# Two mixers' attention normalized on GpSimd before the transposes, values as stationary rows, and the order of work in the first and later mixers changed

## The chip, the cores and the metric

One core of one Trainium2 chip. The metric is device time in microseconds (us) of one launch; its median over several runs is what is compared. A "turn" below is a transpose on TensorE (a matmul against the identity); PSUM banks are written as numbers 0 to 7.

## What is computed

Four layers on 256 rows of width 1,024, in float32. The kernel runs them in one launch:

```python
for layer in range(2):                       # first block
    hn  = rms_norm(x, norm_mix_pre[layer])
    mix = even_mixer(...) if layer == 0 else odd_mixer(...)   # attention + state space; gated recurrence
    x   = x + rms_norm(mix, norm_mix_post[layer])
    x   = x + rms_norm(swiglu(rms_norm(x, ...)), ...)
for i in range(2):                           # second block
    h = _rmsnorm(x, norm_mix[i])
    # i == 0: 8 heads, scores from two parts (128 + 64 wide); i == 1: 8 heads that share 2 key/value heads
    # both: 4 more heads against a memory of 256 rows
    s = q @ k.T ; p = softmax(s * scale) ; out = p @ v
    x = x + concat(mix, mem_out) @ w_out[i]
    x = x + swiglu(_rmsnorm(x, norm_ffn[i]))
```

The change is in the first mixer (its first projection and its state space), in small orders of the second and third, and above all in the attention of the third and fourth mixers: 12 heads each, 256 queries by 256 keys, values 128 wide.

## The kernel before

**Precision and weights.** Every projection is done as three matmuls on rounded parts (`mm3`, L458 to L461): high by high, high input by the weight's rest, and the input's rest by the high weight. Weights come in chunks of 128 x 2,048 (1 MB each) through three buffers RAW (SyncE's queue, `weights`), are rounded by ScalarE into WH (`split_hi`, L1098) and their rest is taken by VectorE into WL (`split_lo`, L1715). `feed(c)` on ScalarE and on VectorE does this for the chunks up to c + 3; where it stands in each engine's program is written by hand. One such feed occupies VectorE for over 2 us.

**Order.** Each engine runs one in-order program (`pe`, `act`, `dve`, `pool`, `sync`), all cross-engine order is by semaphores that the programs wait on. An instruction that waits holds everything behind it on its engine.

**Attention of the third and fourth mixers** (`attention_ahead`, one function in each of `pe`, `act`, `dve`). For each head h:

- TensorE `products(h)` (L759): scores of 256 x 256 into bank h % 2; the third mixer's own heads take two parts, so twice the matmuls.
- VectorE `top(h)` (L2273): the row maxima, negated.
- ScalarE (L1583): the exponentials into P (two buffers), with their row sums into `den`.
- TensorE `turn_p(h)` (L465): P is turned into bank 2 + h % 2.
- VectorE (L2295): the copy of that bank into PT.
- TensorE `pv(h)` (L783): PT by the values; queries are output rows. Four matmuls with 128 columns.
- After each four heads: VectorE `group_divide` (`divide`, L2028 and L2034) divides by the sums into Y, TensorE `finish` turns Y (8 turns for each group), ScalarE copies it rounded (`attn_group`, L1115), VectorE takes the rest (`group_lo`, L1731), and these are the inputs of the output projection `wide_mm`.

TensorE's program for one step of `attend` is `products(h + 2)`, `turn_p(h)`, fill, `pv(h - 1)`. VectorE's is `top(h + 2)`, copy of h, `fill(h)`, and divide or lo where due. The fills are what the rest of the mixer still owes: turns of further queries and keys on TensorE; on VectorE scaled evacuations and feeds (`fill2`: h = 0, 1, 3, 7; `fill3`: h = 0, 1, 3, 7). GpSimd does only the small inverse roots of the norms (`rsqrt`, L2405 and L2407) in this stage.

**First mixer.** `first_edge` does the first projection, beginning when row 0's turned and rounded inputs and the chunk's first quarter are split in both parts. The state space goes in four quarters q: TensorE `b_u(q)`, VectorE `rotate(q)` and `scan(q)` (L1975 to L1997), which ends with two products W, then TensorE `c_h(q)` (L670 to L675) into bank 7, then VectorE `skip(q)` (L1962), which reads bank 7. GpSimd computes CFe from CFo (L2463 to L2470).

Of the kernel before, what the change touches and what calls it, by code (L numbers as in the profile page):

```python
# [212 lines left out]
class Tally:  # L213
# [5 lines left out]
    def up(self):  # L219
# [9 lines left out]
    qk mx ex tp pta ptd pv yt ytp oh ol glua glud  # L229
# [8 lines left out]
              ("n1", 1), ("nk1", 1), ("g0", 8), ("g2", 4), ("g1", 8), ("g3", 8))  # L238
# [4 lines left out]
HSUM = numbered("memk0 n0 nk0 zm qp memk1 n1 nk1")  # L243
# [3 lines left out]
def program(nc, A, PLAN, NCH):  # L247
# [10 lines left out]
    with top:  # L258
# [146 lines left out]
        PD = numbered("R TH a1 a2 a3 a4 a5 THE PH AA AB DEN REC R2 SN CS h1 h2 h3 AB_ CSm p q s FR r u v FI f1 f2 f3 CF")  # L405
# [11 lines left out]
        FFNS = ("ffn0", "ffn1", "ffn2", "ffn3")  # L417
        WHEN = (3, 5, 5, 5, 5, 3, 3, 3)
# [12 lines left out]
        def htlo_n(ed, t, k):  # L431
            return 16 * ed + 8 * t + k + 1
# [24 lines left out]
        def pe(e):  # L457
# [40 lines left out]
            def first_edge():  # L498

                for c in range(2):  # L500
                    for t in range(2):
                        for i in range(4):
                            k = 4 * c + i
                            if t == 0 and c == 0:
                                e.wait_ge(S.lo, i + 1)
                            elif t == 0 and i == 0:
                                e.wait_ge(S.lo1, 1)
                            elif t == 0 and i == 2:
                                e.wait_ge(S.lo, 5)
                            tk = edge_product(0, c, PS[:, t, :], t, k, slice(512 * i, 512 * i + 512))  # L510
                            if c == 0 and t == 0 and i == 0:
                                e.wait_ge(S.c_x1, 16)
                                turn(0, 1, (0,))
                            elif c == 0 and t == 1 and i == 0:
                                turn(0, 1, (1,))
                    tk.then_inc(S.used, 1)
# [144 lines left out]
            def c_h(q):  # L661
                if q == 0:
                    e.wait_ge(S.k0, 1)
                    e.wait_ge(S.pp, PP["CF"])
                else:
                    e.wait_ge(S.ssm, q)
                e.wait_ge(S.w, 2 * q + 2)
                for j in range(4):
                    rows = slice(32 * j, 32 * j + 32)
                    e.matmul(PS[rows, 7, 0:128], K0[rows, q, :], uT[rows, q, 0:256:2], start=True, stop=False)  # L670
                for i in range(4):
                    for j in range(4):
                        e.matmul(PS[32 * j:32 * j + 32, 7, 128:256], CFo[:, i // 2, 4 * q + j, :], W[:, WAT[i], JJ[j], :], start=False, stop=False)
                    for j in range(4):
                        tk = e.matmul(PS[32 * j:32 * j + 32, 7, 1:128], CFe[:, i // 2, 4 * q + j, :], W[:, WAT[i], JJ[j], 0:127], start=False, stop=i == 3)  # L675
                tk.then_inc(S.ch, 1)
# [17 lines left out]
            def attention0():  # L694
# [23 lines left out]
                def pv(h):  # L718
                    e.wait_ge(S.pta, h + 1)
                    if h == 4:  # L720
                        e.wait_ge(S.yt, 2)
# [28 lines left out]
            def attention_ahead(base, heads, P, PT, Y, ready, fill, pvfree, tfree=None):  # L750
# [24 lines left out]
                def pv(h):  # L775
# [4 lines left out]
                    for t in range(2):  # L780
                        b, o = heads[h]["banks"][t], heads[h]["at"]
                        for kt in range(2):
                            tk = e.matmul(PS[:, b, o:o + 128], PT[:, h % 2, kt, 128 * t:128 * t + 128], heads[h]["v"][kt],  # L783
                                          start=kt == 0, stop=kt == 1)
                    tk.then_inc(S.pv, 1)

                def finish(h0):
                    G = (base + h0) // 4
                    for jp in range(2):
                        four(heads[h0]["banks"][jp], Y, jp,  # L790
                             lambda j, t: e.wait_ge(S.yt, 2 * G + t + 1) if j == 0 and jp == 0 else None).then_inc(S.ytp, 1)

                def attend():
                    for h in range(13):
# [7 lines left out]
                        if h in (5, 9):  # L802
                            finish(h - 5)

                return products, attend, finish
# [222 lines left out]
            def tfree2():  # L1028
# [3 lines left out]
            products2, attend2, finish2 = attention_ahead(8, HEADS2, P2, PT2, Y2, ready2, fill2, pvfree2, tfree2)  # L1032
# [5 lines left out]
                    at={0: [lambda: mem_rows(1, mem_free, (0, 1))], 1: [lambda: mem_rows(1, mem_free, (2, 3))]})  # L1038
# [13 lines left out]
            wide_mm(PLAN["out0"], 5, lambda k: (YAh, YAl, OUT0[k // 2] + k % 2), lambda ci: e.wait_ge(S.ol, 3 + ci), lambda: finish2(8))  # L1052
# [30 lines left out]
            products3, attend3, finish3 = attention_ahead(20, HEADS3, P3, PT3, Y3, ready3, fill3, pvfree3)  # L1083
# [6 lines left out]
            wide_mm(PLAN["out1"], 7, lambda k: (YAh, YAl, k), lambda ci: e.wait_ge(S.ol, 9 + ci), lambda: finish3(8))  # L1090
# [3 lines left out]
        def act(e):  # L1094
# [25 lines left out]
            def turn(ed, t, then=None):  # L1120
                name, gi = GAINS[ed]
                ts = slice(128 * t, 128 * t + 128)
                for j in range(2):
                    e.wait_ge(S.turn, turn_n(ed, t, j))
                    for i in range(4):
                        k = 4 * j + i
                        copy(HTh[:, k, ts], PS[:, 4 + 2 * t + j, 128 * i:128 * i + 128], col(name, gi + k)).then_inc(S.hthi, 1)
# [142 lines left out]
            turn(0, 0, lambda j: first_split(j))  # L1270
            first_split(2)
            first_split(3)

            def second_split(j):
                if j == 0:
                    e.wait_ge(S.w1, 16)
                    e.activation(WH[:, 1, 0:1024], RAW[:, 1, 0:1024], ACT.Copy).then_inc(S.hi1, 1)
                    split_hi(1, slice(1024, CH))
                    n_split[0] = 2

            turn(0, 1, second_split)
# [41 lines left out]
            def decay_sines():  # L1323
                e.wait_ge(S.pd, PD["DEN"])
                e.wait_ge(S.fills, 2)
                e.activation(N1, THE, ACT.Abs).then_inc(S.pa, 1)
                e.activation(SN, THE, ACT.Sin).then_inc(S.pa, 1)
                e.wait_ge(S.pa, PA["N1"])
                e.activation(CS, N1, ACT.Sin, bias=hp[:, 0:1], scale=-1.0).then_inc(S.pa, 1)

# [16 lines left out]
            decay_sines()  # L1347
# [362 lines left out]
        def dve(e):  # L1710
# [26 lines left out]
            def turn(ed, t, then=None):  # L1737
                name, gi = GAINS[ed]
                ts = slice(128 * t, 128 * t + 128)
                for j in range(2):  # L1740
                    e.wait_ge(S.hthi, htlo_n(ed, t, 4 * j + 3))
                    for i in range(4):
                        k = 4 * j + i
                        rest(HTl[:, k, ts], PS[:, 4 + 2 * t + j, 128 * i:128 * i + 128], HTh[:, k, ts], col(name, gi + k)).then_inc(S.htlo, 1)
# [136 lines left out]
            turn(0, 0, first_split)  # L1881
            first_split(2)
            first_split(3)

            def second_split(j):
                if j == 0:
                    e.wait_ge(S.hi1, 1)
                    e.tensor_tensor(WL[:, 1, 0:1024], RAW[:, 1, 0:1024], WH[:, 1, 0:1024].bitcast(f32), SUB).then_inc(S.lo1, 1)
                    e.wait_ge(S.hi, 5)
                    split_lo(1, slice(1024, CH))  # L1890
                    n_split[0] = 2

            turn(0, 1, second_split)
# [6 lines left out]
            feed(PLAN["ev_u"][0] - 1)  # L1900
            e.wait_ge(S.pa, PA["SN"])
            e.tensor_tensor(SN, SN, R, MUL).then_inc(S.pd, pd.up())
            e.wait_ge(S.pa, PA["CS"])
# [715 lines left out]
```

## Time and profile before

| | |
|---|---|
| median of 3 runs | 1256.16 us (1255.80 to 1256.63) |
| profiled execution | 1257.03 us, of which the span is 1255.2 us |
| TensorE busy | 1237.0 us, 6,366 matmuls |
| VectorE busy | 810.8 us |
| ScalarE busy | 670.5 us |
| GpSimd busy | 91.0 us |
| granted TensorE clock, mean | 1.000 |

How to read it: busy time is the union of the intervals in which an engine has an instruction in flight, and matmuls overlap, so a matmul's duration is longer than the time it holds TensorE. Between two matmuls of one kind, the distance from start to start is what each costs. A float32 matmul (not rounded) shows as two instructions in the trace, a turn as one. A row of the time line gives start, duration, engine, line, operation, output and inputs, shape, how many like instructions were merged, and in brackets the idle time before it with what ended it.

### The profile page before, as it was taken

How to read it: one execution, taken by the hardware profiler on the slowest of the kernel's cores; microseconds unless marked ns; L12 is line 12 of the kernel's file. 1: busy time of each engine (PE TensorE's matmuls, PEld its weight loads, DVE VectorE, ACT ScalarE, POOL GpSimd, SP SyncE). 2: the span in 40 equal slices, each digit the busy share in tenths (PEclk: the TensorE clock that was granted, in tenths of full speed). 3: DMA queues.
4: the chain of work that ended last, by engine and by line, in shares of the span. 5: the costliest groups of instructions: out<-in, count | busy, mean ns of one | idle time of the engine just before them, and what ended most of it. 6: DMA issues, size and time to landing. Idle time of an engine off the chain costs nothing.

```text
span 1255.2 us, 15794 instructions
## 1 busy us (share of the span) xinstructions
PE 1237.0 (99%) x6366; PEld 1030.9 (82%) x6366; DVE 810.8 (65%) x1034; ACT 670.5 (53%) x981; POOL 91.0 (7%) x121
## 2 busy tenths in 40 slices
PE   7999999999999999999999999999999999999998
PEld 6778888888888888888888888888888888888887
DVE  7995766654787766654687756656547774655553
ACT  7765644433898644443687635444436654544431
POOL 2410100000110100000133100000001200000000
PEclk9999999999999999999999999999999999999999
DMA  7334555555554565555554124555555334555551
GB/s 302 102 116 145 194 188 197 179 191 200 186 200 145 193 219 198 175 194 188 187 201 169 67 102 167 201 186 183 182 192 183 126 102 137 199 182 187 187 183 67
DMA packets 32392, 216.60 MB, mean 173 GB/s; under 512 B 3888, under 2 KB 4272, under 8 KB 7232
## 3 DMA queue, kind: packets, MB, share of 16 engines
q1 hardware_dynamic: 30240, 210.19, 48.5%
q0 software_dynamic: 1360, 4.78, 1.2%
q8 instruction: 50, 0.82, 0.3%
q10 hardware_dynamic: 720, 0.63, 0.2%
q14 instruction: 22, 0.18, 0.0%
HBM read 214.54 MB, written 1.05 MB: 172 GB/s over the span
## 4 chain that ended last, share of the span: by engine, by line
PE 89%; DVE 7%; issue 1%; ACT 1%; POOL 1%; DMA 0%; DVEq 0%; SPq 0%; ACTq 0%
PE PS L459 25%; PE PS L461 25%; PE PS L460 25%; PE PS L465 5%; PE PS L759 2%; DVE WL L1715 1%; PE PS L493 1%; PE PS L496 1%; PE PS L494 1%; PE PS L783 1%; PE PS L533 1%; PE PS L527 1%; PE PS L528 1%; DVE YG L1992 1%; DVE YG L1982 0%
## 5 line engine op out<-in xcount | busy, mean ns | idle before, releaser
L1715 DVE TENSOR_TENSOR WL<-RAW,WH 128x2048 fp32r<-128x2048 f32 (+2 forms) x200 | 443.1, 2218 | 310.9 <-ACT WH L1098 310.9
L1098 ACT ACTIVATE WH<-RAW 128x2048 fp32r<-128x2048 f32 (+2 forms) x200 | 370.7, 1857 | 367.2 <-PE PS L461 367.2
L459 PE MATMUL PS<-WH,HTh 128*128 128x512 f32 (+1 forms) x848 | 334.7, 395 | 0.1
L461 PE MATMUL PS<-WH,HTl 128*128 128x512 f32 (+1 forms) x848 | 329.0, 388 | 0.0
L460 PE MATMUL PS<-WL,HTh 128*128 128x512 f32 (+1 forms) x848 | 328.3, 387 | 0.0
L461 PEld LDWEIGHTS PS<-WH,HTl 128*128 128x128 f32 x848 | 159.2, 188 | 33.2
L459 PEld LDWEIGHTS PS<-WH,HTh 128*128 128x128 f32 x848 | 159.4, 188 | 32.1 <-DVE WL L1715 1.1
L460 PEld LDWEIGHTS PS<-WL,HTh 128*128 128x128 f32 x848 | 159.5, 188 | 30.6
L459 PE MATMUL PS<-WH,YAh 128*128 128x512 f32 x402 | 158.8, 395 | 0.4 <-DVE HTl L1732 0.3
L461 PE MATMUL PS<-WH,YAl 128*128 128x512 f32 x402 | 156.7, 390 | 0.0
L460 PE MATMUL PS<-WL,YAh 128*128 128x512 f32 x402 | 156.5, 389 | 0.0
L459 PEld LDWEIGHTS PS<-WH,YAh 128*128 128x128 f32 x402 | 75.5, 188 | 16.2 <-issue 1.5
L461 PEld LDWEIGHTS PS<-WH,YAl 128*128 128x128 f32 x402 | 75.5, 188 | 15.9
L460 PEld LDWEIGHTS PS<-WL,YAh 128*128 128x128 f32 x402 | 75.6, 188 | 14.9
L2405 POOL TENSOR_SCALAR st<-st 128x2 f32<-128x2 f32 (+4 forms) x33 | 20.2, 611 | 761.4 <-ACT JK L1133 699.3
L459 PE MATMUL PS<-WH,YBh 128*128 128x512 f32 x160 | 62.5, 391 | 0.0
L461 PE MATMUL PS<-WH,YBl 128*128 128x512 f32 x160 | 62.3, 389 | 0.0
L460 PE MATMUL PS<-WL,YBh 128*128 128x512 f32 x160 | 62.3, 389 | 0.0
L1115 ACT ACTIVATE HTh<-PS,cst 128x128 fp32r<-128x128 f32 (+1 forms) x136 | 39.0, 377 | 25.5 <-PE PS L465 25.5
L1732 DVE SCALAR_TENSOR_TENSOR HTl<-PS,cst,HTh 128x128 fp32r<-128x128 f32 (+1 forms) x136 | 38.9, 351 | 14.0 <-ACT HTh L1115 13.9
L2407 POOL TENSOR_TENSOR st<-st,mh 128x2 f32<-128x2 f32 (+4 forms) x33 | 39.6, 1201 | 2.7
L1115 ACT ACTIVATE YAh<-PS 128x512 fp32r<-128x512 f32 x38 | 21.6, 584 | 29.1 <-PE PS L465 29.1
(344 smaller groups left out, 1445.2 us busy)
## 6 DMA issues: line engine op xcount, KB each, us to landing
RAW<-in_w SPq DMA_DIRECT2D x196, 1024.0 KB, 4.9
BC<-in_rows POOLq DMA_DIRECT2D x4, 512.0 KB, 4.0
YG<-in_mem POOLq DMA_DIRECT2D x4, 512.0 KB, 4.9
X<-in_x SPq DMA_DIRECT2D x2, 512.0 KB, 5.6
RAW<-in_w SPq DMA_DIRECT2D x4, 256.0 KB, 5.8
BC<-in_s SPq DMA_DIRECT2D x1, 512.0 KB, 11.8
YG<-in_s SPq DMA_DIRECT2D x1, 512.0 KB, 12.0
BB<-in_s SPq DMA_DIRECT2D x1, 512.0 KB, 12.7
```

Of the source, the lines that this page charges most:

```text
L459: e.matmul(out, ah, bh, start=start, stop=False)
L460: e.matmul(out, ah, bl, start=False, stop=False)
L461: return e.matmul(out, al, bh, start=False, stop=stop)
L465: return e.transpose(out, src, ident[0:p, 0:p])
L493: e.matmul(out, HTh[:, k, ts], WH[:, c % NW, w], start=k == 0, stop=False)
L759: tk = e.matmul(PS[:, h % 2, 256 * t:256 * t + 256], q[:, 128 * t:128 * t + 128], k[:, 0:256], start=i == 0, stop=i == len(parts) - 1)
L1098: e.activation(WH[:, c % NW, w], RAW[:, c % NR, w], ACT.Copy).then_inc(S.hi, 1)
L1115: return e.activation(out, src, ACT.Copy, scale=scale)
L1715: e.tensor_tensor(WL[:, c % NW, w], RAW[:, c % NR, w], WH[:, c % NW, w].bitcast(f32), SUB).then_inc(S.lo, 1)
L1732: return e.scalar_tensor_tensor(out, src, gain, hi.bitcast(f32), MUL, SUB)
L2405: e.tensor_scalar(st[:, at:at + n], st[:, at:at + n], 1e-6, None, ADD).then_inc(S.var, 1)
L2407: e.tensor_tensor(st[:, at:at + n], st[:, at:at + n], mh[:, 0:n], ALU.pow).then_inc(S.rs, 1)
```

## The change

In the attention of the third and fourth mixers:

- VectorE takes the reciprocal of a head's sums at once (12 small ones instead of 3 of four heads each), in its program ahead of `top(h + 2)` and so behind `fill(h - 1)`.
- GpSimd multiplies P of that head (128 x 512) in place by it (`norm`). TensorE's `turn_p(h)` waits for this (`S.pn`) instead of for the exponentials.
- `pv` has the values as the stationary operand and PT as the moving one: two matmuls with 256 columns for four with 128; the output is already turned. `group_divide`, Y and `finish` are gone.
- In the fourth mixer the squares of one group of queries go from ScalarE to VectorE (`memory_squares`), VectorE's feeds there from h = 0, 1, 7 to h = 7 and later.

In the first mixer: the first projection begins with the products that need only the high part, other turns are interleaved, `decay_sines` and `factor` come earlier, `c_h` waits for W half by half and q = 2 uses bank 6, so `skip(2)` moves into the attention. In the second mixer `conv(3)` and `conv_parts(1)` go ahead of a feed and a squares operation; in the third the second half of `mem_rows` goes one step ahead.

```diff
@@ pe
             def first_edge():
-                for c in range(2):
-                    for t in range(2):
-                        for i in range(4):
...
+                for i in range(4):
+                    w = slice(512 * i, 512 * i + 512)
+                    e.wait_ge(S.hthi, htlo_n(0, 0, i))
+                    e.wait_ge(S.hi, i + 1)
+                    e.matmul(PS[:, 0, :], HTh[:, i, 0:128], WH[:, 0, w], start=i == 0, stop=False)
+                    e.wait_ge(S.htlo, htlo_n(0, 0, i))
+                    e.matmul(PS[:, 0, :], HTl[:, i, 0:128], WH[:, 0, w], start=False, stop=False)
...
+                for i in range(4):
+                    e.wait_ge(S.lo, i + 1)
+                    e.matmul(PS[:, 0, :], HTh[:, i, 0:128], WL[:, 0, 512 * i:512 * i + 512], start=False, stop=False)
...
             def c_h(q):
+                b = CH_BANK[q]
                 if q == 0:
                     e.wait_ge(S.k0, 1)
-                    e.wait_ge(S.pp, PP["CF"])
-                else:
-                    e.wait_ge(S.ssm, q)
-                e.wait_ge(S.w, 2 * q + 2)
+                elif q != 2:
+                    e.wait_ge(S.ssm, q - q // 3)
...
+                for n, i in enumerate((0, 3, 1, 2)):
+                    if n % 2 == 0:
+                        e.wait_ge(S.w, 2 * q + 1 + n // 2)
...
                 def turn_p(h):
...
+                    e.wait_ge(S.pn, base - 8 + h + 1)
                     for t in range(2):
-                        e.wait_ge(S.ex, 2 * (base + h) + t + 1)
...
                 def pv(h):
...
-                    for t in range(2):
-                        b, o = heads[h]["banks"][t], heads[h]["at"]
-                        for kt in range(2):
-                            tk = e.matmul(PS[:, b, o:o + 128], PT[:, h % 2, kt, 128 * t:128 * t + 128], heads[h]["v"][kt],
-                                          start=kt == 0, stop=kt == 1)
+                    b, o = heads[h]["banks"][h % 4 // 2], 256 * (h % 2)
+                    for kt in range(2):
+                        tk = e.matmul(PS[:, b, o:o + 256], heads[h]["v"][kt], PT[:, h % 2, kt, :], start=kt == 0, stop=kt == 1)
                     tk.then_inc(S.pv, 1)
-                def finish(h0):
...
-                        if h in (5, 9):
-                            finish(h - 5)
...
             rows_mm(PLAN["qb0"], 3, 3, 512, CQ, (2, 3), qb0_ready,
-                    at={0: [lambda: mem_rows(1, mem_free, (0, 1))], 1: [lambda: mem_rows(1, mem_free, (2, 3))]})
+                    at={0: [lambda: mem_rows(1, mem_free, (0, 1)), lambda: mem_rows(1, mem_free, (2, 3))]})
@@ act
             mem_k(0, (0, 1), KZ)
-            feed(PLAN["mem00"][1])
+            conv_parts(1)
...
+            feed(PLAN["mem00"][1])
             e.wait_ge(S.lamd, 1)
-            conv_parts(1)
...
             def attn_group(base, heads, g, at):
                 for jp in range(2):
-                    attn_out(2 + 2 * ((base - 8) // 4 + g) + jp + 1, heads[4 * g]["banks"][jp], at + 2 * jp)
+                    e.wait_ge(S.pv, base + 4 * g + 2 * jp + 2)
+                    copy(YAh[:, at + 2 * jp:at + 2 * jp + 2, :], pair(heads[4 * g]["banks"][jp])).then_inc(S.oh, 1)
...
-                    e.wait_ge(S.hsq, HSQ["g1"] + 8)
-                    head_norm("g3", two(Zg[3]), 4, 128, "g3")
@@ dve
-            factor()
             table(0)
...
             rotate(3)
-            skip(2)
             scan(3)
...
+            conv(3)
             feed(PLAN["mem00"][0])
-            conv(3)
...
-                for h in range(13):
+                for h in range(12):
+                    e.wait_ge(S.ex, 2 * (base + h) + 2)
+                    e.reciprocal(den[:, :, h:h + 1], den[:, :, h:h + 1]).then_inc(S.rd, 1)
                     if h + 2 < 12:
                         top(h + 2)
...
                     fill(h)
-                    if h % 4 == 0 and h:
-                        group_divide(h // 4 - 1)
-                    elif h in (6, 10):
+                    if h in (6, 10):
                         group_lo(h // 4 - 1)
...
+            def memory_squares(z):
+                sq = BC[:, :].rearrange("p (a b) -> p a b", a=2)
+                e.wait_ge(S.z, ZEV["g3"] + 2)
+                e.wait_ge(S.dv, dv.n)
+                e.scalar_tensor_tensor(sq, z, 1.0 / 128, z, MUL, MUL).then_inc(S.dv, dv.up())
+                e.wait_ge(S.dv, dv.n)
+                e.tensor_reduce(st[:, SO["g3"]:SO["g3"] + 8], sq.rearrange("p a (h d) -> p (a h) d", d=128), AX.X, ADD).then_inc(S.hsum, 1)
             def fill3(h):
-                if h == 0:
-                    feed(PLAN["gqa1"][1])
-                elif h == 1:
-                    feed(PLAN["gqa3"][0])
+                if h == 1:
+                    memory_squares(Zg[3][:, :, :])
                 elif h == 3:
                     scaled("g3", two(Zg[3]), 4, 128)
                 elif h == 7:
-                    feed(PLAN["gqa3"][1])
+                    feed(PLAN["gqa1"][1])
...
+            feed(PLAN["gqa3"][0])
@@ pool
+            def norm(base, P, den, hs):
+                for h in hs:
+                    e.wait_ge(S.rd, base - 8 + h + 1)
+                    e.tensor_tensor(P[:, h % 2, :, :], P[:, h % 2, :, :], den[:, :, h:h + 1].to_broadcast([128, 2, 256]), MUL).then_inc(S.pn, 1)
...
             head_rsqrt("nk1", 8)
+            norm(8, P2, den2, range(12))
...
             head_rsqrt("g1", 8)
+            norm(20, P3, den3, range(4))
             head_rsqrt("g3", 8)
+            norm(20, P3, den3, range(4, 12))
```

## Rows read from the trace of the kernel before

**Rows 1.** The page's first part: busy time, share and instructions of each engine.
```profile
PE 1237.0 (99%) x6366; PEld 1030.9 (82%) x6366; DVE 810.8 (65%) x1034; ACT 670.5 (53%) x981; POOL 91.0 (7%) x121
```

**Rows 2.** Busy time by stretch: span, each engine (instructions), clock, DMA share, GB/s.
```profile
690.00:731.00 41.00, 40.80 (x268) 36.59 (x267) 30.66 (x44) 22.26 (x62) 3.81 (x4) 1.00 0.22 78
1000.00:1031.00 31.00, 29.76 (x218) 26.80 (x216) 26.58 (x38) 20.11 (x70) 2.65 (x2) 1.00 0.30 102
```

**Rows 3.** Time line of TensorE in the fourth mixer's attention: start, duration, instruction.
```profile
1000.78 0.60 PE L465 MATMUL PS<-ident,A3P 128*128 128x128 f32 x4
...
1016.35 1.03 PE L759 MATMUL PS<-KM,QMg 128*128 128x256 f32 x4
1017.21 0.60 PE L465 MATMUL PS<-ident,A3P 128*128 128x128 f32 x4
1017.65 1.06 PE L783 MATMUL PS<-Zg,A3PT 128*128 128x128 f32 x8
1018.54 1.03 PE L759 MATMUL PS<-KM,QMg 128*128 128x256 f32 x4
...
1030.98 0.48 PE L459 MATMUL PS<-WH,YAh 128*128 128x512 f32 x1
```

**Rows 4.** The same of the third mixer's attention.
```profile
698.41 0.60 PE L465 MATMUL PS<-ident,Z 128*128 128x128 f32 x4
...
717.13 0.60 PE L759 MATMUL PS<-KTn,QTn 128*128 128x256 f32 x2
...
718.86 0.60 PE L465 MATMUL PS<-ident,Z 128*128 128x128 f32 x4
...
731.27 0.48 PE L459 MATMUL PS<-WH,YAh 128*128 128x512 f32 x1
```

**Rows 5.** Time line of VectorE in the fourth mixer's attention.
```profile
1012.63 0.19 DVE L2028 RECIPROCAL A3den<-A3den 128x8 f32<-128x8 f32 x1
...
1017.41 0.69 DVE L2273 TENSOR_REDUCE A3M<-PS 128x2 f32<-128x512 f32 x1 [1.46 <-PE PS L759]
1018.02 0.68 DVE L2295 COPY A3PT<-PS 128x512 f32<-128x512 f32 x1
1018.62 1.28 DVE L1731 TENSOR_TENSOR YAl<-PS,YAh 128x512 fp32r<-128x512 f32 x2
...
1021.01 2.28 DVE L1715 TENSOR_TENSOR WL<-RAW,WH 128x2048 fp32r<-128x2048 f32 x1
```

**Rows 6.** Time line of ScalarE: the first of one head's two exponentials.
```profile
1008.50 0.47 ACT L1583 ACTIVATE A3P<-PS,A3M 128x256 f32<-128x256 f32 x1 [0.70 <-DVE A3M L2273]
```

**Rows 7.** Time line of GpSimd: CFe in the first mixer, a root in the fourth.
```profile
33.79 1.05 POOL L2463 TENSOR_TENSOR CFe<-CFo,s 128x512 f32<-128x512 f32 x1 [7.75 <-DVE CFo L1946]
...
37.18 3.10 POOL L2467 TENSOR_TENSOR CFe<-CFo,s 128x512 f32<-128x512 f32 x1
...
1008.05 1.66 POOL L2407 TENSOR_TENSOR st<-st,mh 128x8 f32<-128x8 f32 x1
```

**Rows 8.** Time line of VectorE beside that, and at the end of the last quarter.
```profile
36.53 2.85 DVE L1715 TENSOR_TENSOR WL<-RAW,WH 128x2048 fp32r<-128x2048 f32 x1
...
78.77 0.47 DVE L1962 SCALAR_TENSOR_TENSOR yq<-uT,cst,PS 128x256 f32<-128x256 f32 x1
...
82.74 1.22 DVE L1997 TENSOR_TENSOR W<-YG,SX 128x1024 f32<-128x1024 f32 x1
```

**Rows 9.** Time line of TensorE in the first mixer: first product, and two `c_h`.
```profile
9.30 0.79 PE L493 MATMUL PS<-WH,HTh 128*128 128x512 f32 x1 [2.13 <-DVE WL L1715]
...
51.32 0.43 PE L670 MATMUL PS<-uT,K 32*32 32x128 f32 x8 [1.26 <-DVE W L1997]
...
84.10 0.43 PE L670 MATMUL PS<-uT,K 32*32 32x128 f32 x8 [1.22 <-DVE W L1997]
```

**Rows 10.** Time line of TensorE: one wait each in the second and third mixer.
```profile
360.89 0.36 PE L459 MATMUL PS<-YAh,WH 128*128 128x256 f32 x1 [0.61 <-issue]
...
647.35 0.47 PE L459 MATMUL PS<-WH,YAh 128*128 128x512 f32 x1 [0.33 <-DVE HTl L1732]
```

More of the change, by code:

```diff
@@ L498, in first_edge @@
             def first_edge():
[L500 to L516 removed]
+                for i in range(4):
[5 more added lines that the diff above has]
+                    e.matmul(PS[:, 0, :], HTl[:, i, 0:128], WH[:, 0, w], start=False, stop=False)
+                    if i == 1:
+                        e.wait_ge(S.c_x1, 16)
+                        turn(0, 1, (0,))
+                    elif i == 3:
+                        turn(0, 1, (1,))
@@ L748, in attention0, with attention_ahead @@
                 return finish
-            def attention_ahead(base, heads, P, PT, Y, ready, fill, pvfree, tfree=None):
+            def attention_ahead(base, heads, P, PT, ready, fill, pvfree, tfree=None):
                 def products(h):
@@ L801, in attend @@
                             pv(h - 1)
-                        if h in (5, 9):
-                            finish(h - 5)
-                return products, attend, finish
+                return products, attend
             def gain_turn(src, name, bks, free=None, tiles=4):
@@ L1118, in act, with turn_half, turn @@
                      ("norm_mix_2", 0), ("norm_ffn_2", 0), ("norm_mix_2", 8), ("norm_ffn_2", 8))
-            def turn(ed, t, then=None):
+            def turn_half(ed, t, j):
                 name, gi = GAINS[ed]
                 ts = slice(128 * t, 128 * t + 128)
+                e.wait_ge(S.turn, turn_n(ed, t, j))
+                for i in range(4):
+                    k = 4 * j + i
+                    copy(HTh[:, k, ts], PS[:, 4 + 2 * t + j, 128 * i:128 * i + 128], col(name, gi + k)).then_inc(S.hthi, 1)
+            def turn(ed, t, then=None):
                 for j in range(2):
[L1124 to L1127, printed above, removed]
+                    turn_half(ed, t, j)
                     if then:
@@ L1268, in first_split, with decay_sines @@
                 split_hi(0, slice(512 * i, 512 * i + 512))
[L1270 to L1281, printed above, removed]
+            def decay_sines():
+                e.wait_ge(S.pd, PD["DEN"])
+                e.wait_ge(S.fills, 2)
+                e.activation(N1, THE, ACT.Abs).then_inc(S.pa, 1)
+                e.activation(SN, THE, ACT.Sin).then_inc(S.pa, 1)
+                e.wait_ge(S.pa, PA["N1"])
+                e.activation(CS, N1, ACT.Sin, bias=hp[:, 0:1], scale=-1.0).then_inc(S.pa, 1)
+            turn_half(0, 0, 0)
+            for i in range(4):
+                first_split(i)
+            decay_sines()
+            turn_half(0, 1, 0)
+            turn_half(0, 0, 1)
+            e.wait_ge(S.w1, 16)
+            e.activation(WH[:, 1, 0:1024], RAW[:, 1, 0:1024], ACT.Copy).then_inc(S.hi1, 1)
+            split_hi(1, slice(1024, CH))
+            n_split[0] = 2
+            turn_half(0, 1, 1)
             def angles(q):
@@ L1735, in dve, with turn_half, turn @@
                      ("norm_mix_2", 0), ("norm_ffn_2", 0), ("norm_mix_2", 8), ("norm_ffn_2", 8))
-            def turn(ed, t, then=None):
+            def turn_half(ed, t, j):
                 name, gi = GAINS[ed]
                 ts = slice(128 * t, 128 * t + 128)
+                e.wait_ge(S.hthi, htlo_n(ed, t, 4 * j + 3))
+                for i in range(4):
+                    k = 4 * j + i
+                    rest(HTl[:, k, ts], PS[:, 4 + 2 * t + j, 128 * i:128 * i + 128], HTh[:, k, ts], col(name, gi + k)).then_inc(S.htlo, 1)
+            def turn(ed, t, then=None):
                 for j in range(2):
[L1741 to L1744, printed above, removed]
+                    turn_half(ed, t, j)
                     if then:
@@ L2040, in step @@
                     if h == 2:
+                        skip(2)
                         skip(3)
@@ L2268, in dve, with attention_ahead @@
             two = lambda Z: [Z[:, t, :] for t in range(2)]
-            def attention_ahead(base, heads, M, den, PT, Y, fill, at):
+            def attention_ahead(base, heads, M, den, PT, fill, at):
                 def top(h):
```

122 lines of the change are left out of this document (62 added, 60 removed).

## The prediction

> **What bounds the kernel now.** I read the page's first part, then busy time by stretch, then the time lines of the two attentions. TensorE is busy 1237.0 of 1255.2 us [rows 1]: elsewhere only matmuls that go away, or waits of TensorE, can shorten the kernel. In the attentions TensorE is still busy 40.8 of 41.0 us and 29.8 of 31.0 us, but VectorE has 30.7 and 26.6 us of work there [rows 2], so little need be hung between the two to make a wait. The clock is granted in full in both. The reader should see in [rows 3] how TensorE passes from one head's step to the next without a hole, though each step depends on three engines. It can, because `turn_p(h)` needs only exponentials that were done long before.
>
> **What goes from TensorE.** `finish` is 8 turns; 4 take 0.44 us (1017.21 to 1017.65) [rows 3], so 0.87; three in each mixer, so 2.6 us each, of which the last, 0.87 us, lies in the output projection. `pv` of a head takes 0.89 us (1017.65 to 1018.54) for four matmuls of 128 columns. `products` of a plain head is two matmuls of 256 columns in 0.86 us (1016.35 to 1017.21), and the new `pv` has just that shape: 0.87, a gain of 0.02, 0.5 us over 24 heads. If TensorE stayed the bound, this would be 5.7 us.
>
> **What comes in: a ring.** The reciprocal of head h + 1 stands behind VectorE's copy and fill of head h. GpSimd's multiplication waits for it, `turn_p(h + 1)` waits for that, and the copy of h + 1 waits for the turn. So from turn to turn there is now a closed loop through three engines:
>
> - turn: 0.44 us (1017.21 to 1017.65) [rows 3];
> - to VectorE: 0.20 us, as from the end of the products at 1017.21 to the maximum at 1017.41 [rows 3, 5];
> - copy: 0.60 us (1018.02 to 1018.62) [rows 5];
> - VectorE's fill of that head, D;
> - reciprocal: 0.19 us for 8 columns [rows 5], with its handover 0.25;
> - multiplication on GpSimd: 1.05 us for the same 128 x 512 with a broadcast operand [rows 7], with handover 1.15 (0.10 is my estimate, of the size of the handover to ScalarE).
>
> Sum 2.64 us + D. TensorE's own work for a head is 0.86 + 0.44 + 0.87 = 2.17 in the fourth mixer and for the third mixer's memory heads; its own heads have products of 1.73 us (717.13 to 718.86) [rows 4], so 3.04. A plain head therefore stalls 0.5 us even without a fill, the two last heads of each mixer, which have no products ahead, 1.3 us, and every fill on VectorE enters in full unless products or turns cover it. Before, the copy of h was wanted only after `products(h + 2)` and `turn_p(h + 1)`, which hid D.
>
> The fills are: a feed 2.2 us, a pair of scaled evacuations or rests 1.2 us [rows 5], two operations of `memory_squares` on 1,024 columns, half a feed each and some 0.1 over, 2.4 us.
>
> I laid out both attentions head by head in this way, each engine in its program's order, with 1.05 us for a head's exponentials, two of 0.47 and the reading of their sums [rows 6] (0.91 before ScalarE is free for its next), and an operation of VectorE with two SBUF inputs excluding one of GpSimd. The same layout of the old programs gives 731.2 and 1030.9 us for the start of the output projections; the trace has 731.27 and 1030.98 [rows 3, 4]. For the new programs the distances from turn to turn are:
>
> - Fourth mixer, from head 0: 2.8, 5.0 (squares), 2.6, 4.6 (scaling of g3, 1.2, behind GpSimd's root, which follows `norm` of head 3: 0.3 and 1.66 us [rows 7]), 3.0 and 2.8 (TensorE or ScalarE last), 3.8 (rests), 4.8 (feed), 2.6, 2.6, 3.8 (rests), and 2.2 to the projection: 40.9 us. Before: 1000.78 to 1030.98, 30.2 us. So +10.7, less the `finish` of 0.87 in the projection: **+9.8 us**.
> - Third mixer: 3.8, 6.0 (evacuations and feed), 3.0, 5.0 (feed), 3.0, 3.0, 4.0, 4.8 (feed), 3.0, 2.8, 3.8, 2.2: 44.7 us, beginning 0.5 later since head 0 also has to be multiplied. Before: 698.41 to 731.27, 32.9 us. +12.4 less 0.87: **+11.5 us**.
>
> ScalarE's loss of the squares in the fourth mixer is worth nothing then, for ScalarE no longer comes last. The later feeds there reach the projection in time: a wide chunk is 24 matmuls, over 5 us, and VectorE needs 2.2 for one. SyncE's loads wait for those feeds too; the load for the projection's fourth chunk starts some 25 us later and by the layout is still almost 30 us ahead of its use.
>
> What the lock costs is the open point. The row shows it: beside a feed GpSimd's operation takes 3.10 us for 1.05 and the feed 2.85 for 2.28 [rows 5, 7, 8]; the CFe of 33.79 ran in 1.05 while VectorE multiplied from PSUM. The Trainium skill ("SBUF — State Buffer", section "SBUF: two separate sides") calls the pair of ports that VectorE and GpSimd share an exclusive lock, held for a whole instruction, against VectorE operations with two SBUF inputs or in a two-port mode. By that rule, the trace agrees, the maxima and copies from PSUM don't block `norm`; if they did, `top(h + 2)` would stand ahead of it, 0.6 us a head, and the sum would be up to 24 x 0.6 = 14 us higher.
>
> **First mixer.** TensorE's first product waits 2.13 us for a quarter's WL part [rows 9]; it will start when the WH part is there, one split and its handover earlier, 1.2 us (bounds 0 and 2.1). The five waits of this stage in front of `c_h` and `b_u` are 1.26 at q = 0, 1.22 at q = 3 [rows 9], and three smaller between them. They end with VectorE's chain, which loses `skip(2)`, 0.47, and gives its first W product 1.14 us before the second (of 1.22) [rows 8]; it starts 1.2 earlier with TensorE, and gets back some 0.5 from the lock, since `factor` has moved out from ahead of CFo and GpSimd is further on when the feed comes. 1.2 + 0.5 + 0.5 + 1.1 = **-3.3 us**; bounds 0 (the chain takes it back elsewhere) and -4.9 (the start and all five waits, the smaller put at 1.2 together).
>
> **Second and third mixer.** The two waits, 0.61 and 0.33 us by their rows [rows 10], go with the dividing of the parts earlier and the turns of memory rows earlier: **-1.0 us** with their handovers; bounds 0 and -1.3. The feed that `conv(3)` passes is wanted only by the second gate product, over 2 us later, and this hides it.
>
> **Sum.** 11.5 + 9.8 - 3.3 - 1.0 = +17.0 us. The profiled execution would go from 1257.0 to 1274.0 (span 1272.2); it lies 0.9 us above the median, so the median goes from 1256.2 to **1273.2 us**.
>
> **Rivals.**
>
> - *The ring never closes in time to matter* (faster). Then TensorE stays the bound: -5.7, and -4.3 from the mixers, and some 1 us of old waits in the attentions that a shorter program sheds: 1245 us. For it: TensorE is at 99%, and GpSimd is idle in the stage [rows 2]. Against it: it needs 2.64 + D to be under 2.17. Were GpSimd's multiplication as short as 0.45 us, the same layout still gives +11. Chance 0.07.
> - *The gains just pay* (within 0.2%): would need the multiplication far below any row and the first mixer at its best. 0.02.
> - *A lighter ring.* At 0.7 us for the multiplication the layout gives +15.2 in the attentions, with the mixers' -4.3 1267 us. 0.07.
> - *A heavier ring.* GpSimd's operation at 1.3 us (some heads meeting a longer VectorE operation than I laid out, as CFe at 37.18 did [rows 7]): +25.9, 1278 us; with nothing gained in the first mixer 1281. 0.08.
> - *The clock falls in the attentions*: so far it is 1.00 there with waits of up to 1 us, and the new waits reach 3.9. At the low level a head's 2.17 us become 4.3 and the ring no longer hides it; if half the heads ran so, some +20: 1293 us. 0.02. The Trainium skill ("TensorE: Matmul & The Clock Gate", Part 1) says that an idle array falls back to 1.2 GHz; by it a stretch with enough holes would do this, and no row here shows a fall.
> - My forecast: 0.74.
>
> **Range and chances.** Low end 1265 (lighter ring, best first mixer), high end 1281. What is left out is the faster and the clock's case and tails, under 0.2. Slower by over 0.2% (2.5 us, about what a measurement can tell from no change): 0.74 + 0.07 + 0.08 + 0.02 = 0.91; same 0.02; faster 0.07.
>
> **What would show it.** In the profile after, the turns of P (L465) should stand 2.6 us apart in the plain heads at the end of the fourth mixer, each with a wait put down to GpSimd; GpSimd 24 operations of 1.05 to 1.1 us, more only beside a feed; TensorE's busy time lower by about 6 us and the span longer. The attentions should take 41 and 45 us for 30 and 33. `c_h` should be without waits for q = 0 to 2 and begin the last quarter some 3 us earlier. If the turns follow at 2.2 us, the ring is wrong; if it is right and the sum off, D or the handovers are.

## The result, and the profile after

The changed kernel takes 1282.03 us (median; 1279.18 to 1283.59) against 1256.13 us, a ratio of 1.0203 (95% interval 1.0184 to 1.0223): slower by 25.9 us, where +17.0 was forecast, and 1.0 us above the range. The profiled execution took 1283.59 us, the longest of its runs; its span is 1281.8 us.

From the page of the changed kernel: busy time of the engines (against [rows 1]), the granted clock in 40 slices, and the chain that ended last.

```profile
span 1281.8 us, 15514 instructions
...
PE 1241.4 (97%) x6222; PEld 1028.8 (80%) x6222; DVE 807.5 (63%) x1042; ACT 668.7 (52%) x965; POOL 114.4 (9%) x145
...
PEclk9999999999999999999999999999999989999999
...
PE 91%; DVE 5%; POOL 2%; issue 1%; DMA 1%; ACT 0%; SPq 0%; DVEq 0%; ACTq 0%
```

TensorE has 144 matmuls less and yet 4.4 us more busy time, where 6 less were forecast. Less work that takes longer is a sign to look at the clock, and one slice has it at 8.

The waits of TensorE for GpSimd (all time, times, longest):

```profile
PE PS L467 <- POOL Z L2446: 14.6, 8, 3.7
PE PS L467 <- POOL A3P L2446: 13.6, 9, 2.5
```

These are the turns of P, which wait for the multiplication in the third mixer (Z) and the fourth (A3P). One head of the third mixer, on its time line:

```profile
701.15 2.28 DVE L1722 TENSOR_TENSOR WL<-RAW,WH 128x2048 fp32r<-128x2048 f32 x1
703.35 0.16 DVE L2296 RECIPROCAL A2den<-A2den 128x2 f32<-128x2 f32 x1
...
703.59 1.04 POOL L2446 TENSOR_TENSOR Z<-Z,A2den 128x512 f32<-128x512 f32 x1 [5.05 <-DVE A2den L2296]
...
704.77 2.79 PE L467 MATMUL PS<-ident,Z 128*128 128x128 f32 x12 [3.74 <-POOL Z L2446]
705.90 0.69 DVE L2303 COPY Z<-PS 128x512 f32<-128x512 f32 x1 [1.80 <-PE PS L467]
706.50 0.16 DVE L2296 RECIPROCAL A2den<-A2den 128x2 f32<-128x2 f32 x1
```

This is the ring of the prediction: fill, reciprocal, 0.24 us later the multiplication of 1.04, 1.18 us after its start the turn, then copy and the next reciprocal. The groups of instructions by line (busy time, mean ns of one, idle time before them) show that the multiplications do so on average:

```profile
L2446 POOL TENSOR_TENSOR Z<-Z,A2den 128x512 f32<-128x512 f32 x12 | 12.5, 1042 | 36.8 <-DVE A2den L2296 36.8
L2446 POOL TENSOR_TENSOR A3P<-A3P,A3den 128x512 f32<-128x512 f32 x12 | 12.5, 1042 | 34.4 <-DVE A3den L2296 34.4
```

The parts of the kernel, from the first turn of P to the output projection, against [rows 3, 4]:

| | before | forecast | after |
|---|---|---|---|
| third mixer | 32.9 | 44.7 | 48.9 (694.79 to 743.71) |
| fourth mixer | 30.2 | 40.9 | 45.5 (1012.79 to 1058.26) |

So 8.8 us lie in the two attentions, of 9.6 that are missing in the profiled execution (1274.0 forecast). Busy time by stretch (against [rows 2]; columns: span, then PE, PEld, DVE, ACT and POOL, each with its instructions, then granted clock, DMA share, GB/s), first the two attentions and one part of the third mixer's, then five shorter stretches:

```profile
694.00:744.00 50.00, 35.41 (x172) 29.08 (x170) 27.21 (x45) 17.35 (x53) 12.11 (x12) 0.90 0.18 64
...
714.00:731.00 17.00, 12.90 (x72) 11.05 (x73) 9.84 (x18) 6.10 (x20) 5.21 (x5) 1.00 0.23 70
1012.00:1059.00 47.00, 33.34 (x155) 26.50 (x154) 26.31 (x44) 18.84 (x56) 13.99 (x14) 0.89 0.07 23
...
60.00:70.00 10.00, 8.90 (x56) 6.89 (x53) 9.79 (x11) 7.09 (x10) 5.05 (x9) 0.83 0.50 157
700.00:712.00 12.00, 8.26 (x34) 7.03 (x33) 6.10 (x11) 3.22 (x11) 2.08 (x2) 0.72 0.26 87
738.00:748.00 10.00, 7.61 (x29) 6.29 (x30) 3.10 (x6) 1.19 (x2) 1.04 (x1) 0.83 0.01 2
1025.00:1035.00 10.00, 7.66 (x36) 6.39 (x34) 4.15 (x10) 4.83 (x14) 3.12 (x4) 0.83 0.01 2
1042.00:1060.00 18.00, 12.16 (x47) 9.63 (x48) 9.72 (x17) 4.32 (x12) 4.17 (x4) 0.81 0.23 67
...
701.00:703.00 2.00, 0.04 (x1) 0.00 (x0) 2.00 (x2) 0.00 (x0) 0.00 (x0) 1.00 0.00 0
704.00:710.00 6.00, 5.22 (x19) 4.72 (x20) 0.86 (x3) 2.28 (x6) 1.67 (x2) 0.50 0.52 175
```

The clock records of this trace hold two levels only, 1.00 and 0.50, so a mean of 0.72 over 12 us is 6.7 us at the 1.2 GHz level (0.50), 0.83 over 10 us is 3.4 us, 0.81 over 18 us is 6.8 us: together 20 us in or at the end of the attentions. The last two rows show one case: TensorE does next to nothing from 701 to 703 and the clock is still 1.00; from 704 to 710 it works at 0.50. In the kernel before the clock was 1.00 in both attentions [rows 2].

The first mixer after, against [rows 9], by the time line of TensorE: the first product, and the `c_h` of q = 0 and q = 3.

```profile
8.08 0.77 PE L506 MATMUL PS<-WH,HTh 128*128 128x512 f32 x1 [0.99 <-ACT WH L1104]
...
48.63 0.43 PE L680 MATMUL PS<-uT,K 32*32 32x128 f32 x8
...
81.58 0.43 PE L680 MATMUL PS<-uT,K 32*32 32x128 f32 x8
```

The product starts 1.2 us earlier, and neither `c_h` waits. By the next edge's turn of X TensorE is 2.5 us ahead (128.35 to 125.84), though a stretch at the low level (60 to 70 us, above) lies in between.

### The profile page after: what moved, and what is told of

Read it like the earlier page. It is cut to its first block, busy times and chain, and to the rows that moved or that the text cites. A ratio compares the mean times of both kernels' runs of the same rounds, so it can differ in the third digit from the quotient of the medians.

```text
span 1281.8 us, 15514 instructions
## 1 busy us (share of the span) xinstructions
PE 1241.4 (97%) x6222; PEld 1028.8 (80%) x6222; DVE 807.5 (63%) x1042; ACT 668.7 (52%) x965; POOL 114.4 (9%) x145
## 3 DMA queue, kind: packets, MB, share of 16 engines
HBM read 214.54 MB, written 1.05 MB: 168 GB/s over the span
## 4 chain that ended last, share of the span: by engine, by line
PE 91%; DVE 5%; POOL 2%; issue 1%; DMA 1%; ACT 0%; SPq 0%; DVEq 0%; ACTq 0%
PE PS L461 25%; PE PS L463 25%; PE PS L462 25%; PE PS L467 6%; PE PS L775 1%; PE PS L498 1%; PE PS L496 1%; PE PS L798 1%; PE PS L495 1%; PE PS L544 1%; PE PS L538 1%; PE PS L539 1%; DVE WL L1722 1%; POOL A3P L2446 1%; POOL Z L2446 1%
## 5 line engine op out<-in xcount | busy, mean ns | idle before, releaser
L462 PEld LDWEIGHTS PS<-WL,HTh 128*128 128x128 f32 x848 | 159.9, 189 | 30.7
L1739 DVE SCALAR_TENSOR_TENSOR HTl<-PS,cst,HTh 128x128 fp32r<-128x128 f32 (+1 forms) x136 | 38.7, 352 | 10.6 <-ACT HTh L1121 10.6
L462 PEld LDWEIGHTS PS<-WL,YBh 128*128 128x128 f32 x160 | 30.0, 188 | 6.2
## 6 DMA issues: line engine op xcount, KB each, us to landing
BC<-in_s SPq DMA_DIRECT2D x1, 512.0 KB, 11.5
```

The source lines that it names most:

```text
L462: e.matmul(out, ah, bl, start=False, stop=False)
L1739: return e.scalar_tensor_tensor(out, src, gain, hi.bitcast(f32), MUL, SUB)
```

## The experiments

Theory: the ring is priced rightly, and what was left out is the clock, which the waits bring down. Rivals: the ring's own steps are dearer than the rows said; GpSimd's multiplication or its ports are the cost, wherever the reciprocal stands; the new product or the moved fills cost time themselves.

The kernel before was measured again beside each group of experiments (medians 1256.31 to 1256.82 us), and each ratio below is against that. In the diffs `...` stands for lines that are not shown.

**Work in TensorE's waits.** In `turn_p`, with a count for each head:

```diff
+                    for n in range(WARM[base][h]):
+                        e.matmul(PS[:, b, :], HTh[:, 0, 0:128], HTh[:, 0:2, :], start=True, stop=True)
                     e.wait_ge(S.pn, base - 8 + h + 1)
```

> The changed kernel with 80 additional matmuls of 128 x 512 columns whose results nobody reads (0.23 us each at the full clock, 18 us in all), put where TensorE waits for the multiplied exponentials, each group a little shorter than its wait. Theory (the ring is priced rightly, and the missing 9 us are the stretches at the 1.2 GHz level that the waits bring about): the clock stays at 1.00 in both attentions, turn to turn 45 and 41 us as in the prediction, and the time falls by about 9 us to 1273 us although TensorE has more to do. Rival (the clock's fall has another cause, or the 9 us are dearer handovers in the ring): 1282 us or above, with the low stretches where they were.

Measured: 1273.09 us (1272.69 to 1274.43), ratio 1.0133 (1.0118 to 1.0148). The two attentions by stretch, with the granted clock third from the end:

```profile
693.00:740.00 47.00, 44.33 (x226) 36.25 (x226) 27.91 (x46) 17.57 (x53) 11.82 (x12) 1.00 0.19 68
1007.00:1050.00 43.00, 40.01 (x203) 31.51 (x202) 26.66 (x45) 17.98 (x53) 13.40 (x13) 1.00 0.07 25
```

(There are 94 added matmuls, 22 us of them, and not the 80 and 18 us that the expectation counts.) The clock is 1.00 in both, and from the first turn to the projection they take 44.7 and 40.9 us, the lengths of the prediction. TensorE has 22 us more to do and the kernel is 8.9 us shorter: so much of the change's loss is the clock's. In the profiled executions the difference is 10.6 us: 8.8 in the two attentions, 1.3 in the first mixer, where the changed kernel's execution had a low stretch and this one had none, though no matmul was added there, and 0.4 between the attentions, where the projection after the changed kernel's first one begins at the low level. So part of the 8.9 us may come from the first mixer; the medians don't tell how much.

Two more kernels divide the waits between them: the same edit, with matmuls only in the six waits of 2.2 us and more, and only in the shorter ones of 0.5 to 1.7 us (nine waits and 35 matmuls; the expectation counts eleven and 40).

> The changed kernel with the additional matmuls in the six long waits alone (heads 2, 4 and 11 of the third mixer, 4, 8 and 11 of the fourth; 2.2 to 3.7 us each), 59 matmuls. Theory A (a single long wait brings the clock down): no stretch at the 1.2 GHz level is left in the attentions, 1273 to 1274 us. Theory B (it is the share of waits over several heads): the short waits of 1.2 to 1.7 us still bring some stretch, 1275 to 1279 us.

> The changed kernel with the additional matmuls in the eleven shorter waits alone (0.5 to 1.7 us), 40 matmuls, the long waits left empty. Theory A: the low stretches stay as they are, 1281 to 1283 us. Theory B: part of them goes, 1275 to 1280 us.

Measured: 1273.47 us (1273.32 to 1274.97) with the long waits filled, 1281.37 us (1280.97 to 1283.54) with the short ones filled. By stretch, first two rows of the former, then three of the latter:

```profile
693.00:740.00 47.00, 40.30 (x208) 33.18 (x209) 27.91 (x46) 17.39 (x52) 11.65 (x12) 1.00 0.20 68
1007.00:1050.00 43.00, 35.29 (x183) 27.73 (x182) 26.36 (x45) 18.02 (x53) 13.37 (x13) 1.00 0.07 25
```

```profile
705.00:711.00 6.00, 5.98 (x20) 5.19 (x21) 0.76 (x2) 2.29 (x6) 1.04 (x1) 0.50 0.39 161
1029.00:1032.00 3.00, 3.00 (x12) 2.72 (x11) 0.75 (x2) 1.99 (x5) 1.04 (x1) 0.52 0.00 0
1046.00:1049.00 3.00, 3.00 (x11) 2.45 (x10) 0.99 (x2) 1.35 (x5) 0.95 (x1) 0.51 0.39 164
```

So it is the long waits that matter (theory A), though not every one of them did it (see the last section): with them empty the low stretches stay where they were, whether the short ones are filled or not.

**The place of the reciprocal.** VectorE's program in the changed kernel is, for each head, reciprocal(h), maximum(h + 2), copy(h), fill(h). First only the fill is taken out of the ring:

```diff
                         e.tensor_copy(PT[:, h % 2, :, :], PS[:, 2 + h % 2, :].rearrange("p (t k) -> p t k", t=2)).then_inc(S.ptd, 1)
+                    if h + 1 < 12:
+                        over(h + 1)
                     fill(h)
```

where `over(h)` is the wait for the exponentials and the reciprocal, no longer at the head of the loop; `over(0)` stands ahead of the loop.

> The changed kernel with the reciprocal of head h + 1 taken right behind the copy of head h, ahead of the fill: the loop stays one head long, only D goes out of it. Theory (loop 2.64 us + D): the turns stand 2.6 us apart in plain heads and wherever a fill was alone responsible, the layout gives +6.2 us in the third mixer's attention and +5.2 in the fourth's against the kernel before, with the mixers' -4.0 us 1263.5 us, up to 4 us more if a stretch at the 1.2 GHz level comes in. Rival (the fills cost by VectorE's time, not by their place): nothing is gained beyond the clock's 9 us, 1273 us.

Measured: 1266.75 us (1266.06 to 1268.05), ratio 1.0085 (1.0069 to 1.0101). Turns of P in two plain heads of the fourth mixer:

```profile
1021.87 0.63 PE L467 MATMUL PS<-ident,A3P 128*128 128x128 f32 x4 [0.50 <-POOL A3P L2451]
...
1024.56 0.63 PE L467 MATMUL PS<-ident,A3P 128*128 128x128 f32 x4 [0.34 <-POOL A3P L2451]
```

They stand 2.69 us apart, the ring without D (forecast: 2.64), and the attentions take 41.1 and 37.6 us. Not all of D is gone, though: the feed now follows the reciprocal at once, and GpSimd's multiplication meets it. From the same time line:

```profile
1025.91 2.27 DVE L1722 TENSOR_TENSOR WL<-RAW,WH 128x2048 fp32r<-128x2048 f32 x1
1026.07 3.01 POOL L2451 TENSOR_TENSOR A3P<-A3P,A3den 128x512 f32<-128x512 f32 x1 [1.65 <-DVE A3den L2294]
...
1029.22 0.70 PE L467 MATMUL PS<-ident,A3P 128*128 128x128 f32 x4 [2.31 <-POOL A3P L2451]
```

Three multiplications take 3.01 us here and one 1.94, where the changed kernel has 1.04 in all 24. The two longest waits of TensorE, 2.30 and 2.31 us, stand each behind one of the three, and behind each of the two begins a low stretch of 3.4 us (the clock is 0.83 from 1025 to 1035 us and from 704 to 714). Such a stretch costs at most half its length, 1.7 us, so the clock could account for the 3.3 us above the layout; no run here parts it from the stretched multiplications.

Next, the reciprocal a whole head earlier, but ahead of the fill, with `over(1)` before the first copy:

```diff
-                    if h + 1 < 12:
-                        over(h + 1)
+                    if h + 2 < 12:
+                        over(h + 2)
                     fill(h)
```

> The changed kernel with one thing moved: VectorE takes the reciprocal of head h + 2 right behind its copy of head h, ahead of the fill, instead of the reciprocal of head h + 1 behind copy and fill. Theory (the loop copy, fill, reciprocal, multiplication, turn is what costs): a head's chain then has two heads' time, the same layout gives +0 us in the third mixer's attention and +2 in the fourth's against the kernel before, the clock stays full, and with the -4.0 us of the mixers 1254 us (1250 to 1258). Rival (GpSimd's multiplication itself, through the ports it shares with VectorE or by its length, is what costs): it is still needed 24 times, so no more than a third of the loss goes, 1272 us or above.

Measured: 1256.09 us (1253.89 to 1257.8), ratio 0.9997 (0.9988 to 1.0007): 26 us back, and the rival that GpSimd is the cost wherever the reciprocal stands has fallen. The attentions take 33.1 and 33.8 us. Here one sees what was left. From this kernel's time line:

```profile
1019.45 0.17 DVE L2294 RECIPROCAL A3den<-A3den 128x2 f32<-128x2 f32 x1 [0.49 <-ACT A3P L1592]
1019.54 2.27 DVE L1722 TENSOR_TENSOR WL<-RAW,WH 128x2048 fp32r<-128x2048 f32 x1
1019.70 3.01 POOL L2453 TENSOR_TENSOR A3P<-A3P,A3den 128x512 f32<-128x512 f32 x1 [2.00 <-DVE A3den L2294]
```

With the feed right behind the reciprocal, GpSimd's multiplication takes 3.01 us for 1.04: it does not get on until VectorE's feed is over, at 1021.8. There are three of these, and two more of 1.96 and 1.41 beside the squares and the scaling. This is what the Trainium skill says ("SBUF — State Buffer", section "SBUF: two separate sides") of an exclusive lock that VectorE operations with two SBUF inputs take against GpSimd; the trace agrees. A second cost stands in this kernel: the reciprocal ahead of the fill makes VectorE wait for the exponentials first, 13.2 us of such waits in the two attentions, against 6.6 in the next kernel. No run parts the two.

So the reciprocal belongs a head earlier *and* behind the fill, where a maximum and a copy from PSUM follow it:

```diff
                     fill(h)
                     if h in (6, 10):
                         group_lo(h // 4 - 1)
+                    if h + 2 < 12:
+                        over(h + 2)
```

> The changed kernel with the reciprocal in the place that it has, behind copy and fill of head h, but of head h + 2 instead of head h + 1. Theory: a chain then has two heads' time less what VectorE still has queued, and VectorE never waits for exponentials ahead of a fill, which cost the version with the reciprocal ahead of the fill its places with 3.8 to 5.1 us; the layout gives -1.5 and -1.2 us in the two attentions against the kernel before, with the mixers' -4.0 us 1249.5 us. Rival (a fill of 2.2 us or more stands before the reciprocal again and delays it): 1254 us or above.

Measured: 1248.69 us (1248.27 to 1249.06), ratio 0.9938 (0.9924 to 0.9952). The attentions take 31.6 and 29.6 us. From its time line:

```profile
702.93 1.04 POOL L2453 TENSOR_TENSOR Z<-Z,A2den 128x512 f32<-128x512 f32 x1 [0.80 <-DVE A2den L2294]
703.35 0.68 DVE L2308 COPY Z<-PS 128x512 f32<-128x512 f32 x1
...
703.95 2.28 DVE L1722 TENSOR_TENSOR WL<-RAW,WH 128x2048 fp32r<-128x2048 f32 x1
```

The copy from PSUM runs beside the multiplication without stretching it, and the feed begins when it is nearly over.

Then three feeds are moved as well (third mixer's from heads 1 and 3 to 2 and 4, fourth's from 7 to 4):

```diff
                     scaled_out("nk1", ZA, (4, 5))
+                elif h == 2:
                     feed(PLAN["mem11"][1])
-                elif h == 3:
+                elif h == 4:
                     feed(PLAN["qb1"][0])
...
-                elif h == 7:
+                elif h == 4:
                     feed(PLAN["gqa1"][1])
```

> As the one before it, and three fills of VectorE moved so that no two of them meet and none stands beside ScalarE's own: two feeds of the third mixer's attention from heads 1 and 3 to heads 2 and 4, the fourth's from head 7 to head 4. Theory: -2.6 and -2.3 us in the two attentions by the layout, 1247.5 us in all, below the kernel before and below the version with the mixers' reordering alone (1251.8 us). Rival (the moved feeds delay the projection's weights): 1249 to 1252 us.

Measured: 1246.99 us (1246.38 to 1248.45), ratio 0.9927 (0.9914 to 0.9940): faster than both kernels. The attentions take 30.7 and 28.5 us. Its page:

```profile
span 1244.5 us, 15514 instructions
...
PE 1228.8 (99%) x6222; PEld 1019.8 (82%) x6222; DVE 807.9 (65%) x1042; ACT 668.7 (54%) x965; POOL 114.7 (9%) x145
```

With the same instructions as the changed kernel TensorE is busy 12.6 us less than there, with the clock at 1.000 in the mean, and 8.2 less than before the change [rows 1].

**Without the division.** The reciprocals and the multiplications are left out.

```diff
-                    e.wait_ge(S.pn, base - 8 + h + 1)
+                    e.wait_ge(S.ex, 2 * (base + h) + 2)
...
-            norm(8, P2, den2, range(12))
...
-            norm(20, P3, den3, range(4))
...
-            norm(20, P3, den3, range(4, 12))
```

> The changed kernel without the division by the sums in the second and third attention (the third and fourth mixer): no reciprocal and no multiplication, and the turn of the exponentials waits for the exponentials alone, as before; that part of the computation is left out. Theory: TensorE is the bound again; the layout gives -2.9 and -4.6 us in the two attentions against the kernel before, with -4.0 us of the mixers 1245 us and no stretch of the low clock there. Rival (the new shape of the values' product, or the fills moved, cost time themselves): above 1252 us.

Measured: 1245.18 us (1244.96 to 1246.3), ratio 0.9911 (0.9896 to 0.9926). The attentions take 30.8 and 26.6 us. The new product and the moved fills cost nothing that shows; the loss came with the place of the division and the waits that it made, and the version above comes within 2 us of having none.

**The mixers' reordering alone.** Against the changed kernel, all that belongs to the attention of the third and fourth mixers is as before, and the rest is kept. One part of the edit:

```diff
-                    b, o = heads[h]["banks"][h % 4 // 2], 256 * (h % 2)
-                    for kt in range(2):
-                        tk = e.matmul(PS[:, b, o:o + 256], heads[h]["v"][kt], PT[:, h % 2, kt, :], start=kt == 0, stop=kt == 1)
+                    for t in range(2):
+                        b, o = heads[h]["banks"][t], heads[h]["at"]
+                        for kt in range(2):
+                            tk = e.matmul(PS[:, b, o:o + 128], PT[:, h % 2, kt, 128 * t:128 * t + 128], heads[h]["v"][kt],
+                                          start=kt == 0, stop=kt == 1)
```

> The kernel before with the reordering of the first and the later mixers alone, and the old attention. Theory: the marks of the changed kernel hold, -2.4 us in the first mixer and -1.6 in the second and third: 1252.1 us. Rival (the gain is lost behind, since the attentions have their own bound): 1254 to 1256 us.

Measured: 1251.80 us (1251.67 to 1253.28), ratio 0.9966 (0.9953 to 0.9979), 4.8 us below the kernel before on the same chip. TensorE is 3.7 us ahead at the end of the first mixer (128.35 to 124.67) and another 1.6 at the third mixer's first turn of P. The attentions keep their 32.9 and 30.2 us.

## Why the prediction missed, point by point

- **The ring** was right in mechanism and in size. The steps measured 1.04 for the multiplication (1.05 taken), 0.16 for the reciprocal (0.19), 2.69 to 2.74 from turn to turn in plain heads (2.64), and with the clock held up the attentions took 44.7 and 40.9 us, as laid out head by head: none of the 24 distances there is more than 0.15 us from the forecast one. (The distances that the prediction lists add up to 0.3 us less than its 44.7 and 40.9; that is within their rounding.)
- **D, the fills in the ring**, was right in the kernel with the clock held up: in the fourth mixer the turn behind a feed came 4.84 us after the one before, behind the rests 3.83, behind the squares 5.03, against 2.61 to 2.74 in plain heads. Taking the fills out gave 3.6 and 3.3 us in the two attentions (44.7 to 41.1, 40.9 to 37.6), where the layout had 5.3 and 4.6 (11.5 less 6.2, 9.8 less 5.2). That run is no clean measure of D: each attention has a low stretch of 3.4 us in it, which can cost up to 1.7, and beside the feeds the lock stretches the multiplication.
- **`finish`**: the projection's part was priced at 0.87 us; from the projection's start to the next attention's first turn the distance falls from 269.5 to 268.7, 0.8.
- **The lock** did not touch the changed kernel, as the prediction said: the multiplications took 1.04 us, beside maxima and copies from PSUM. It was only a matter of order: 3.01 us with a feed right behind the reciprocal.
- **First mixer**: -3.3 forecast, -2.9 to -4.1 measured in the eight kernels whose clock stayed full there (-2.5 in the profile of the changed kernel, with a low stretch in it). **Second and third mixer**: -1.0 forecast with a bound of -1.3, -1.6 measured; with the 0.5 us that head 0's multiplication adds before the first turn, -1.1. Small misses in sizes.
- **The clock** is the step that failed. It stood among the rivals with a chance of 0.02 and was kept out of the sum and of the range, on the ground that no row showed a fall. But no wait of TensorE in the attentions before was over 0.9 us, while the same sentence of the prediction says that the new ones reach 3.9. That a program without such waits shows no falls said nothing of a program with them. The rule of the Trainium skill named there ("TensorE: Matmul & The Clock Gate", Part 1) spoke for a fall; the trace agrees, with 0.50 from 704 to 710 us behind a wait of 3.74. That the clock also fell with waits of 2.24 to 2.54 us, and did not behind one of 2.70, the rows of this case alone show. Its price was wrong as well, in the other direction: +20 us, from half of all heads at the low level. Measured it was 8.9 us in the medians, 8.8 of the attentions in the profiled executions: some 20 us of time at the low level, not half of 94, each of which costs at most half its length, and less where TensorE waits in it anyway. With 9 us for it in the sum the forecast would have been 1282.
- **The heavier ring** (1278 to 1281 us) would have given nearly the measured time, and a reader of the median alone might take it for the cause. The multiplication's 1.04 us and the kernel with filled waits exclude it.
- Of the signs named in the prediction, 24 multiplications of 1.04, waits put down to GpSimd and `c_h` without waits came out; the last quarter's `c_h` begins 2.5 us earlier, for some 3. The turns in the plain heads at the end of the fourth mixer stand 3.7 and 2.9 us apart in the changed kernel, with a low stretch up to 1048 us in both distances, and 2.73 and 2.61 where the waits are filled. The sign that went the other way, TensorE's busy time "lower by about 6 us", is the one that told of the clock: it rose by 4.4. In the fastest kernel, which has the same instructions, it is 8.2 lower.

## What to carry to other kernels

When work is put between two engines that alternate, write down the loop from a buffer's use to its next, with everything queued in it, and start the new step one turn of the loop earlier than it is needed: here that was worth 33 us for an index of 2 in the place of 1, some 9 of them by the clock. When a forecast contains new waits of TensorE as long as these (2.2 to 3.7 us), put a fall of the clock into the sum and not among the unlikely rivals. Right behind the handover to GpSimd, let VectorE do what it reads from PSUM, and its long operations on two SBUF operands before or well after.

## What the runs showed of the hardware

Long waits of TensorE brought the clock down. Five of the changed kernel's six waits of 2.2 to 3.7 us have a stretch at the 1.2 GHz level begin in them or less than 1 us behind them, one of 6.8 us behind the wait of 3.74 and four of 3.4 us behind those of 2.24 to 2.54; 59 matmuls in those six waits, of which nobody uses the results, gave back 8.6 us by the medians, 8.4 of it in the attentions by the profiled executions. Filling the shorter waits changed 0.7 us, within the spread of the two kernels' runs. Not every long wait is followed by a fall: the third mixer's head 4 waited 2.7 us, and the clock was 1.00 from 714 to 731 us. A low stretch also came in the first mixer, between 60 and 70 us, in the profiles of the changed kernel and of the one with its short waits filled, and in none of the other nine. It has no long wait ahead of it (0.42 and 0.61 us in the changed kernel, while others had 1.02 and 0.60 at the same place and kept the full clock); what brings it about was not tried. The times of the changed kernel's four runs fall from 1283.6 to 1279.2 us as their mean clock rises from 0.990 to 0.995; a lower share of 0.005 over 1,280 us is 6.4 us at most, so the clock can account for this spread.
